# Moving router logits, state products and a modulation slab between a layer's out-projection and its first expert

## The reference

```
mod = silu(c) @ w_mod + b_mod;  sh1, sc1, gt1, sh2, sc2, gt2 = split(mod)
h   = rms_norm(x, g_mix) * (1 + sc1) + sh1
mix, states, histories = token_mixers(h)      # 4 retention heads, depthwise convolution
x   = x + gt1 * (mix @ w_out)
h   = rms_norm(x, g_ffn) * (1 + sc2) + sh2
ff  = grouped_moe(h)
x   = x + gt2 * ff
```

## Time and profile before

| | |
|---|---|
| runs (us) | 1498.44, 1498.92, 1502.77; median 1498.92 |
| profiled execution | 1498.92 us, span 1497.0 us, mean granted clock 0.978 |
| busy | TensorE 1425.7 us (95%), VectorE 678.9 (45%), ScalarE 239.8 (16%), GpSimd 104.7 (7%) |
| transfers | 501.93 MB, 335 GB/s on average; SP's queue holds 82.7% of the 16 engines' span |
| in 40 slices | 409 to 410 GB/s through most of both expert loops |

### The profile page before, as it was taken

How to read it: one execution, slowest core, us unless ns; L and a number is a source line. 1 busy time by engine, 2 the same in 40 slices (tenths; PEclk the granted TensorE clock), 3 DMA queues, 4 the chain that set the end, 5 groups by cost and what they waited for, 6 DMA issues and landing times.

```text
span 1497.0 us, 19640 instructions
## 1 busy us (share of the span) xinstructions
PE 1425.7 (95%) x6993; PEld 660.9 (44%) x6994; DVE 678.9 (45%) x1986; ACT 239.8 (16%) x392; POOL 104.7 (7%) x149
## 2 busy tenths in 40 slices
PE   6999998999999999999989999989999999999996
PEld 3777664333333233333337766633333323333333
DVE  2697646333333333333347965553343323234333
ACT  1201311111110111111131123211111101111112
POOL 1071111000000000000001611100000000000000
PEclk9899996999999999999999999989999999999998
DMA  9944558999999974999998355589999999799992
GB/s 332 355 159 148 226 219 312 393 410 409 409 410 410 410 302 159 391 410 410 409 409 341 132 202 228 211 328 410 410 410 409 410 410 409 308 397 410 410 409 76
DMA packets 131314, 501.93 MB, mean 335 GB/s; under 512 B 8635, under 2 KB 8955, under 8 KB 131266
## 3 DMA queue, kind: packets, MB, share of 16 engines
q1 hardware_dynamic: 127056, 487.84, 82.7%
q0 software_dynamic: 3600, 11.21, 2.3%
q10 hardware_dynamic: 626, 2.46, 0.6%
HBM read 495.32 MB, written 7.00 MB: 336 GB/s over the span
## 4 chain that ended last, share of the span: by engine, by line
PE 62%; SPq 24%; DMA 5%; DVE 4%; issue 3%; ACT 1%; PEld 0%; PEldq 0%; ACTq 0%; DVEq 0%
PE ps L386 58%; SPq L356 21%; PE ps L389 3%; DMA ring<-in_w_mod 3%; DMA ring<-in_w_exp_up 2%; SPq L368 1%; DVE arena L1017 1%; SPq L311 1%; ACT arena L829 1%; SPq L359 0%; PEld ps L386 0%; ACT L829 0%; ACT hT L829 0%; DVE hT L1224 0%; DVE rt L1279 0%
## 5 line engine op out<-in xcount | busy, mean ns | idle before, releaser
L386 PE MATMUL ps<-ring,arena 128*64 128x512 f32 x3360 | 754.6, 599 | 17.5 <-DMA ring<-in_w_exp_up 12.9
L386 PEld LDWEIGHTS ps<-ring,arena 128*64 128x64 f32 x3360 | 233.0, 137 | 479.7 <-issue 425.5
L829 ACT ACTIVATE arena<-ps 128x512 f32<-128x512 f32 (+3 forms) x240 | 129.8, 551 | 831.3 <-PE ps L386 742.8
L386 PE MATMUL ps<-hT,ring 128*128 128x288 f32 x1024 | 256.2, 412 | 7.1 <-DVE hT L1091 4.2
L1380 DVE SCALAR_TENSOR_TENSOR xT<-ps,mod,xT 128x256 f32<-128x256 f32 x280 | 133.0, 475 | 254.8 <-PE ps L386 254.8
L386 PE MATMUL ps<-arena 64*128 64x288 f32 (+6 forms) x1212 | 234.1, 485 | 10.6 <-DVE arena L1347 4.7
L386 PEld LDWEIGHTS ps<-hT,ring 128*128 128x128 f32 x1024 | 196.7, 193 | 64.9 <-DVE hT L1091 4.7
L386 PEld LDWEIGHTS ps<-arena 64*128 64x128 f32 (+6 forms) x1212 | 99.8, 167 | 161.9 <-issue 145.6
L1122 DVE SCALAR_TENSOR_TENSOR arena<-arena,wcT 128x256 f32<-128x256 f32 x240 | 123.6, 577 | 1.6
L829 ACT ACT_TABLE_LOAD x49 | 62.9, 1283 | 314.7 <-PE ps L386 292.3
L1414 DVE TENSOR_TENSOR arena<-ps,arena 128x512 f32<-128x512 f32 x35 | 24.2, 691 | 163.1 <-PE ps L386 163.1
(11 more groups left out here) (169 smaller groups left out, 578.5 us busy)
## 6 DMA issues: line engine op xcount, KB each, us to landing
ring<-in_w_exp_gate SPq DMA_DIRECT2D x128, 1024.0 KB, 16.6
ring<-in_w_exp_up SPq DMA_DIRECT2D x128, 1024.0 KB, 17.7
ring<-in_w_exp_down SPq DMA_DIRECT2D x128, 1024.0 KB, 17.5
ring<-in_w_mod SPq DMA_DIRECT2D x48, 1024.0 KB, 8.8
ring<-in_w_in SPq DMA_DIRECT2D x24, 1024.0 KB, 21.5
ring<-in_w_out SPq DMA_DIRECT2D x8, 1024.0 KB, 12.8
big<-in_state_ret POOLq DMA_DIRECT2D x4, 512.0 KB, 10.4
arena<-in_state_ret POOLq DMA_DIRECT2D x4, 512.0 KB, 5.2
```

The source lines that it names most:

```text
L386: return nc.tensor.matmul(out, lhsT, rhs, start=start, stop=stop, skip_group_check=True)
L829: return nc.scalar.activation(out, in_, f, **kw)
```

## The change

- **Roots.** ScalarE takes the root straight from PSUM (`sqrt(sum / n + eps)`), VectorE inverts it afterwards (`inverse`); the scaling on VectorE is gone. This holds for the norms at the layer starts, the second norm, the convolution's norm, the group norms and the final norm.
- **Squares.** VectorE adds squares 0 to 6 of the second norm during out-projection (`add_square`), TensorE multiplies that sum and the last square by ones.
- **States.** The sample values stand one head below the other on 128 partitions (vS, kdS). One GpSimd operation masks them for all heads. `sample_states(g)` runs four matmuls, one head each, in four groups of 32 rows, behind out-projection's blocks 4 and 6; `add_states(g)` adds them. The four stores follow the second of these.
- **Router.** `w_router` is stationary and hT moves, feature block by feature block; the logits come out transposed in three column groups, VectorE copies them to `lgT`, and TensorE turns them.
- **Routing.** The softmax is not divided by its sum, masking with −1 and copies are gone, the counts of blocks come from comparisons with a table (`thr`) and their starts from another (`below`); `sel0` comes directly after the positions, the weights after the slots.
- **Gate-2 slab.** On TensorE from before the logits to behind the h2 transposes; ScalarE's copy from before the exponential to behind the h2 copies; VectorE's addition last.
- Some semaphores are shared, and the constants have 320 columns more.

The diff, cut to its core:

```
@@ TensorE
-                def head_states(i):
-                    hp = slice(STATE_ORDER[i] * P, (STATE_ORDER[i] + 1) * P)
-                    pe.wait_ge(V.vmask_ready, i + 1)
-                    if i >= 2:
-                        pe.wait_ge(V.snew_ready, i - 1)
-                    for g in range(2):
-                        last = mm(ps[:, STATE_BANKS[i % 2][g], :], kd[0:NS, 2, hp], vmasks[i % 2][0:NS, g * 512:(g + 1) * 512],
-                                  True, True)
+                def sample_states(g):
+                    for h in range(H):
+                        hr = slice(h * NS, (h + 1) * NS)
+                        last = mm(ps[:, STATE_BANK[h], :], kdS[hr, :], vmask[hr, g * 512:(g + 1) * 512], True, True)
                     last.then_inc(V.snew_done, 1)
...
                     out_block(m, RET_K).then_inc(V.outproj_done, 1)
+                    if m == 4:
+                        pe.wait_ge(V.vmask_ready, 1)
+                        pe.wait_ge(V.mod2_added, 3)
+                        sample_states(0)
+                    elif m == 6:
+                        pe.wait_ge(V.snew_ready, 1)
+                        sample_states(1)
...
-                feature_sum(7, sq2, KC, arrived=V.norm2_sq).then_inc(V.norm2_sum, 1)
-                pe.wait_ge(V.mod2_added, 3)
-                head_states(0)
-                head_states(1)
-
+                pe.wait_ge(V.norm2_acc, 1)
+                mm(ps[:, 7, 0:T], ones, sq2[:, 0, :], True, False)
+                pe.wait_ge(V.norm2_sq, KC)
+                mm(ps[:, 7, 0:T], ones, sq2[:, KC - 1, :], False, True).then_inc(V.norm2_sum, 1)
                 pe.wait_ge(V.x_mid, KC)
-                mod_slab(6, 1, layer_load(2))
-                pe.drain().then_inc(V.mod2_done, 1)
-                for t, (t0, m) in enumerate(TILES):
-                    for k in range(KC):
-                        if t == 0:
-                            pe.wait_ge(V.h2_ready, k + 1)
-                        last = mm(ps[0:m, 4, t * E:(t + 1) * E], hT[:, k, t0:t0 + m], wr[:, k, :], k == 0, k == KC - 1)
+                for k in range(KC):
+                    pe.wait_ge(V.h2_ready, k + 1)
+                    for t, (t0, m) in enumerate(TILES):
+                        last = mm(ps[32 * t:32 * t + E, 4, 0:m], wr[:, k, :], hT[:, k, t0:t0 + m], k == 0, k == KC - 1)
                 last.then_inc(V.logits_done, 1)
...
+                        if n == 1:
+                            pe.wait_ge(V.lgT_ready, 1)
+                            tr(ps[:, 5, 0:96], lgT[0:96, :], 96).then_inc(V.lg_trans, 1)
-                pe.wait_ge(V.h2_copied, 6)
-                head_states(2)
-                head_states(3)
+                mod_slab(6, 1, layer_load(2))
+                pe.drain().then_inc(V.mod2_done, 1)
@@ VectorE
-            def inverse_var(ch, dst, src, n):
-                ch.link(v.tensor_scalar(dst, src, 1.0 / n, EPS, ALU.mult, ALU.add))
-                v.reciprocal(dst, dst).then_inc(V.var_ready, 1)
+            def inverse(ch, buf, nth):
+                dve.wait_ge(V.rstd_ready, nth)
+                ch.link(v.reciprocal(buf, buf))
...
+                for m in range(4, KC):
+                    add_gated(ch, lambda m: OUT_BANK[m % 4], M_GT1, V.outproj_done, V.x_mid, [m])
+                    if m == 4:
+                        for j in range(1, 4):
+                            ch.link(add_square(j))
+                        add_states(0)
+                    elif m == 6:
+                        ch.link(add_square(4))
+                        ch.link(add_square(5))
+                        add_square(6).then_inc(V.norm2_acc, 1)
+                        add_states(1)
@@ GpSimd
-                for i, h in enumerate(STATE_ORDER):
-                    if i >= 2:
-                        pool.wait_ge(V.snew_done, i - 1)
-                    gp.tensor_tensor(vmasks[i % 2][0:NS, :].rearrange("p (b e) -> p b e", b=B),
-                                     vt[0:NS, 2, h * P:(h + 1) * P].unsqueeze(1).to_broadcast([NS, B, DH]),
-                                     C("smask")[0:NS].unsqueeze(2).to_broadcast([NS, B, DH]), ALU.mult).then_inc(V.vmask_ready, 1)
-                for i, h in enumerate(STATE_ORDER):
-                    pool.wait_ge(V.snew_ready, i + 1)
-                    pool.dma_start(dstate(rets_v, h), state(h)).then_inc(V.states_stored if i < 2 else V.Sa_stored, 16)
+                gp.tensor_tensor(vmask.rearrange("p (b e) -> p b e", b=B), vS.unsqueeze(1).to_broadcast([P, B, DH]),
+                                 C("smask").unsqueeze(2).to_broadcast([P, B, DH]), ALU.mult).then_inc(V.vmask_ready, 1)
+                pool.wait_ge(V.snew_ready, 2)
+                for h in (2, 3, 0, 1):
+                    pool.dma_start(dstate(rets_v, h), state(h)).then_inc(V.states_stored if h >= 2 else V.Sa_stored, 16)
@@ ScalarE
-                act.wait_ge(V.var_ready, 3 + H)
-                root(stat[:, 1, :])
+                act.wait_ge(V.norm2_sum, 1)
+                root(stat[:, 1, :], 7, D)
                 shifted(M_SH2, V.h2_scaled, V.h2_ready)
-                act.wait_ge(V.mod2_done, 4)
-                a(kd[:, 1, :], ps[:, 6, :]).then_inc(V.mod2_evac, 1)
                 act.wait_ge(V.lg_ready, 1)
                 a(rt[:, 1, :], rt[:, 0, :], ACT.Exp).then_inc(V.ex_ready, 1)
```

More of the change, by code:

```diff
@@ L68, in constants @@
     c["fold"] = fold.reshape(P, -1)
+    c["eps"] = np.full((P, 1), EPS)
     scale = DH ** -0.5
@@ L796, in _ @@
                     mod_slab(2, 0, layer_load(PRE[0] + E))
[L797 removed]
+                    pe.drain().then_inc(slab_step, 1)
                 pe.wait_ge(V.x_end, 4)
@@ L883, in _ @@
                             a(vt[0:m, t, :], ps[0:m, bank, :]).then_inc(V.v_copied, 1)
+                        for h in range(H):
+                            last = a(vS[h * NS:(h + 1) * NS, :], ps[0:NS, 5, h * P:(h + 1) * P])
+                        last.then_inc(V.v_copied, 1)
                     if n == 11:
@@ new lines, in _ @@
+                iota = C("iota")
+                for t in range(3):
+                    last = v.tensor_scalar(sel[:, t, :], iota[:, 0:BLK], 1000.0, slot0[:, t:t + 1], ALU.add, ALU.is_equal)
+                last.then_inc(V.sel0_ready, 1)
+                nsubs, starts = rt[:, 14, 0:E], rt[:, 14, E:2 * E]
+                dve.wait_ge(V.cnt_done, 1)
+                above = mixed[:, 0:E * (MAXSUB - 1)].rearrange("p (e s) -> p e s", e=E)
+                tt(above, bl(ps[:, 4, 0:E], MAXSUB - 1), C("thr").rearrange("p (e s) -> p e s", e=E), ALU.is_gt)
@@ new lines, in _ @@
+                ch.link(v.tensor_reduce(starts, before, AX.X, ALU.add))
+                ch.link(v.scalar_tensor_tensor(r3(13), bc(starts, 3), float(BLK), pos, ALU.mult, ALU.add))
+                for k in range(2):
+                    v.tensor_tensor(r3(3 + 4 * k), r3(13), r3(8 + k), ALU.mult).then_inc(V.dchain, 1)
+                    ch.n += 1
+                dve.wait_ge(V.dchain, ch.n)
+                for k in range(2):
+                    last = v.tensor_reduce(slots[:, k, :], r3(3 + 4 * k), AX.X, ALU.add)
@@ L1325, in _ @@
+                last.then_inc(V.route_ready, 1)
                 tt(col(12), col(11), col(2), ALU.add)
@@ L1344, in _ @@
-                ch.link(v.tensor_scalar(slot0, slot0, -1000.0, None, ALU.add))
-                iota = C("iota")
-                for t in range(3):
-                    last = v.tensor_scalar(sel[:, t, :], iota[:, 0:BLK], slot0[:, t:t + 1], None, ALU.is_equal)
-                last.then_inc(V.sel0_ready, 1)
-                cnt, nsubs, ends, prev = rt[:, 14, 0:E], rt[:, 14, E:2 * E], rt[:, 14, 2 * E:3 * E], rt[:, 12, 0:E]
-                ch.link(v.tensor_scalar(nsubs, cnt, float(BLK), 1.0, ALU.is_gt, ALU.add))
@@ L1360, in _ @@
-                tt(ends, ends, nsubs, ALU.subtract)
-                ch.link(v.scalar_tensor_tensor(r3(13), bc(ends, 3), float(BLK), r3(13), ALU.mult, ALU.add))
-                for k in range(2):
-                    tt(r3(3 + 4 * k), r3(13), r3(8 + k), ALU.mult)
-                    ch.link(v.tensor_reduce(slots[:, k, :], r3(3 + 4 * k), AX.X, ALU.add))
-                v.memset(rtmp[:, :, :], 0.0)
-                dve.wait_ge(moe_open, l + 1)
-                v.memset(selT, 0.0).then_inc(V.selT_copied, 1)
```

262 lines of the change are left out of this document (127 added, 135 removed).

## The result

Seven runs of the changed kernel took 1483.02 to 1488.20 us, median 1485.23; seven of the kernel before 1491.37 to 1502.77, median 1498.44. The ratio is 0.9928 with a 95% interval of 0.9901 to 0.9955: faster by 0.7%, or 10.8 us (the medians alone differ by 13.2), where 7.9 us were forecast. The profiled execution took 1485.71 us, its span is 1483.9 us, 13.1 less than before.

A forecast was written before the change was run, and what follows sets the result against it. Weight transfers in the expert loop were taken as the bound. Layer 1 −2.7, layer 0 −4.65 and the end −0.5 gave −7.9 us, from 1498.92 to 1491.0 us; range 1485.5 to 1502.

The forecast's parts named there:

- The bound: Expert loop: weight transfers at 410 GB/s bound it, so a layer ends a fixed time after its weights start flowing.
- the rival with TensorE as the bound: An earlier start of the weight stream gains nothing, only costs of 5.65 less 0.5 stay: 1504 us; chance 0.07.
- Second norm and sample rows: After out-projection: norm gains 3.8 us, sample rows 1.9, so hT's last row comes 8.4 after t0 instead of 14.1.
- Gate-2 slab: Behind the h2 transposes it lets expert 0's first up load leave 16.2 us after t0, 7 later than before.
- the rival on the clock: TensorE keeps 2.4 GHz through the gate-2 slab, up load at 13.8, 2.4 us less per layer: 1486 us; chance 0.12.
- Restart: Moment from which expert weights act as flowing unbroken: 38.4 us after t0, against 48.1 (layer 0) and 44.5 (layer 1).
- State products: Two sets of four matmuls inside out-projection: 1.2 us each, 2.4 per layer, delaying t0; out-projection's sooner start gives back 1.0.
- the rivals with products one behind another: State matmuls don't overlap: 7.4 us per layer, 1501 us, chance 0.14; at the lower clock 9.8, 1506 us, chance 0.08.
- t0: The end of the last x_mid block in each layer; forecast to come 1.4 us later per layer.
- Stores: State stores (2.1 MB) go out at t0; rival: they stay beside the loads, 5.1 us per layer, 1501 us, chance 0.07.
- Layer starts: Reciprocal behind the root delays in-projection by 3.65 us in layer 0 and 2.0 in layer 1; nothing later gives them back.
- End: At the kernel's end one scaling of 0.46 us goes: −0.5.

The follow-up runs named there:

- the run with fills: Changed kernel plus seven chained 512-column fills (about 3.9 us) on VectorE behind the exponential, in the routing chain; 1488.74 us, ratio 0.9933.
- the early root: Changed kernel with ScalarE's root at both layer starts put ahead of the slab evacuations; 1483.79 us, ratio 0.9906.
- the first four experiments: On the changed kernel: gate-2 slab ahead of the logits, 1477.61 us; the early root, 1483.79; both edits, 1478.04; the run with fills, 1488.74.

## Why the prediction held, step by step

- *The bound.* Held: the end follows the restart at a distance that varies by 1.4 us at most, and the rival with TensorE as the bound, where only the costs stay, fell.
- *Second norm and sample rows* (parts 1, 2): 3.9 where 3.68 was forecast; 0.42 and 0.43; last row 8.5 instead of 8.4.
- *Gate-2 slab* (part 4): the term that was mis-sized. 25 transposes were priced at layer 0's 0.213, the first products at 1.9. In time this is some 60% of the rival on the clock, 1.5 us per layer, 3 in all, but not for its reason: out-projection didn't keep the clock up. TensorE waited 4.6 us for the norm, and the logits and the first transposes ran at 0.50, that is 1.2 GHz (layer 1, 951 to 956); then the clock rose, and most of the other 20 transposes (2.85 us) and the whole slab ran at 1.00, 2.4 GHz (958 to 963). So the logits ended at 9.5 instead of 9.0, the slab began at 13.5 instead of 14.3, its first products took 1.24, and the up load left at 14.7 and 14.8, not 16.2.
- *Restart* (part 5): 22.3 behind the up load, as forecast (22.2); no starving; 37.0 instead of 38.4 for the reason just given. That the routing's saving buys nothing in this order was right: the run with fills gave some 5 us per layer of it away free. That the late slab is the price was right too, but moving it ahead returned 2.7 and 6.0 at the restart for loads that leave 12.3 us sooner: expert 1's gate issue then decides, behind a TensorE that lost its clock while idle, and the state stores hold back the loads.
- *State products* (part 6): 1.14 per set, forecast 1.2; the rivals with products one behind another fell. Counted from in-projection, t0 moved by 0.6 in layer 0 and 2.1 in layer 1, not 1.4: the sets and their hand-overs cost 2.5, and in layer 1 out-projection's sooner start was worth 0.4 instead of 1.0.
- *Stores*: out from t0 on and through before the up loads leave, and the weights flow at 405 GB/s afterwards; that rival fell in this order of the slab.
- *Layer starts* (part 7): +4.0 for 3.65 in layer 0, +1.2 for 2.0 in layer 1. "Nothing later gives them back" held in layer 0, where the early root won 4.6 us at t0. In layer 1 it holds only if GpSimd's loads don't move along.
- *End*: −0.5 was forecast; 2.6 went in the two profiled executions, 1.7 of it with the clock at the end of the one of before, a term that the prediction doesn't have. One execution of before can't tell whether it belongs to the change; the interval of the ratio (6.7 to 14.8 us) can't either.

The median of 1485.23 lies 0.3 us below the stated range, the ratio's estimate 0.9928 x 1498.92 = 1488.1 inside it. The forecast was 73% of the 10.8 us. By layer −4.65 and −2.7 were forecast and −5.5 and −5.0 came in the profiled executions: the mechanism was right, and most of what is missing is the clock, at the slab and at the end.

## What to carry to other kernels

Where transfers bound a long stretch, find the moment from which they flow without break, and price each edit by what it does to that moment: here a first block that came 13 us sooner in layer 1 moved it by 7.5, since a slab in the way of the loads had become the last to come. When loads are let go sooner, look at what else moves by then, as the state stores did here. When an edit starts one engine sooner, list the transfers that wait for the same signal; an early norm gained nothing until GpSimd's loads were held back. An instruction that fills TensorE's idle time may be worth its place for the clock of those behind it.

## What the runs showed of the hardware

- The same kernel takes 1491 to 1504 us, and the time goes with the mean clock that it is granted. Of nine runs of the kernel before, beside the first four experiments, the one at a mean clock of 0.983 took 1491.66 us and the one at 0.973 took 1504.28. And 3.6 us of matmuls put into a wait of 4.2 made the gather behind it 1.4 us shorter.
- Four matmuls of 32 rows each in four row groups take 1.14 us where four in one group took 3.69, and x_mid comes only 1.26 us later for it. By the rule that a change of tiling mode drains TensorE (the Trainium skill, "TensorEngine Tiling (Array Packing)", Key Properties) each set has a change to these groups and one back. No row shows them alone: 0.12 us are left for both beside the 1.14, and 0.34 if the products by themselves take the 0.92 of a full overlap, an estimate (3.69/4).
- Transfers of GpSimd's queue take a large part of the bandwidth from SP's loads while both run: a copy and two loads 1.47 MB against 2.24 MB in 10 us, the state stores and a load 2.06 MB against 1.26 MB in 12 us, where both queues together moved only 278 GB/s.
